# A 16-row bias product in the place of two zero products at the head of a two-layer trunk

## The chip, the cores and the metric

The kernel runs on one core of one Trainium2 chip, as one launch. The metric is the device time in microseconds (us); several executions of the same program are timed and the median stands for it. One more execution is recorded by the hardware profiler, and all rows of the trace come from that one. The core has a matrix engine (TensorE, PE in the rows; PEld is its weight load), VectorE (DVE), ScalarE (ACT), GpSimd (POOL) and SyncE (SP). Each has a queue of its own and waits on semaphores for the others. SyncE and ScalarE can both issue transfers from main memory.

## What is computed

256 tokens of width 1024 go through two layers in float32. Layer 0 has a stick-breaking attention and a SwiGLU. Layer 1 has an attention in three dilated groups over one shared set of keys and values, with a relative bias, and a SwiGLU. Cut to what the change touches:

```python
def shared_kv_from(x, g_kv, w_kv):
    kv = (rms_norm(x, g_kv) @ w_kv).reshape(b, s, N_GROUPS, 2, N_HEADS, HEAD_DIM)
...
def dilated_group_attention(qb, kk, vv, rel_bias, window, dilation):
    rel = Q_BLOCK + i - m
    bias = rel_bias[relative_bucket(rel * dilation)]
    bias = jnp.transpose(bias, (2, 0, 1))[:, None].astype(jnp.float32)
    s = jnp.einsum('brhnqd,brhnkd->brhnqk', qb.astype(jnp.float32), kk.astype(jnp.float32)) * scale + bias
    s = jnp.where(valid, s, NEG_INF)
    lse = jax.nn.logsumexp(s, axis=-1)
...
def reference(x, ...):
    for layer in range(DEPTH):
        h = rms_norm(x, g[0])
        h = mixer_a(...) if layer < N_A_LAYERS else mixer_b(...)
        x = x + rms_norm(h, g[1])
        h = swiglu(rms_norm(x, g[2]), w_gate_up[layer], w_down[layer])
        x = x + rms_norm(h, g[3])
```

`rel_bias` is a table of 32 buckets by 16 heads. The bias is needed in layer 1 only, whose attention begins near 310 us.

## The kernel before

**Staging.** Weights stream through three buffers (`raw`, "units" of up to 1 MB) that SyncE fills. ScalarE cuts each unit to its high part (`hi`, line 511, into `w_hi`), VectorE makes the rest (`lo`, line 800, into `w_lo`), and PE multiplies high by high, high by low and low by high, so that a float32 product becomes three fast ones. SyncE may load unit s only when unit s-3 is cut. The order on each engine is written out by hand; no scheduler changes it.

**The bias.** A one-hot matrix `select_in` (32 buckets by 512 distances) and the table `rel_in` (32 by 16) are loaded; one product on PE (line 1572, 16 by 512 in float32) picks the bias by head and distance, VectorE copies it to `bias_out` (line 1107), and GpSimd stores it to memory in two transfers (lines 482, 483), from where it is read back per head much later.

**The head of the program**, in the order of each engine:

- SyncE loads the identity `eye` (375), the two tiles of x (377), the first query and key weights (378 to 380), the first value unit (`half_values_a(0, 0)`), `ones` (382), the one-hot matrix (383) and the table (384), then two small matrices (385, 386) and further weights. The transfer of the second value unit waits for the first columns' products of the query, and the next query unit for those of the key.
- ScalarE loads the norm gains (705, 64 rows) and the gain of the shared norm (706, 8 rows), loads its function table (708), scales half of the turned x by the gains (713), rounds it (725) and then cuts units.
- PE multiplies zeros (`keep_busy(4)`, line 1551) from the moment that `rows` is cleared, turns tile 0 of x (1563), turns the gains (1560, after a wait for both gain transfers), turns tile 1, computes the first query and key columns straight from the float32 weights (`first_columns`, 1243), spreads the norm factors over rows (`spread_rows`, 1219), waits for the bias transfers, runs the bias product (1572), and goes on with the values (`values_a`, 1268 to 1271), the first scores (`scores_a`, 1252 and 1253), more values, the next query and key (`project_a`, 1197 to 1199) and the running sums of the attention (`sums_a`, 1285).
- VectorE squares x (1087), scales its half of the turned x (1080), makes the low part of x (1098), a diagonal (871), the first low weight part (800), the norm rows (876), query and key (921, 922), a second low part, and the bias copy (1107). An attention step has lines 900 to 905 there (its last, 905, is what `sums_a` waits for) and line 579 first on ScalarE, which waits for the scores.
- GpSimd computes the norm factors (422, 425) and then waits for `bias_out`.

The bias product writes to bank 3 of the PSUM memory, which the gains' transpose used before it and the scores use after it. Each bank holds 512 float32 columns, and the zero products write to bank 2, as the values do.

Of the kernel before, what the change touches and what calls it, by code (L numbers as in the profile page):

```python
# [32 lines left out]
NH = 16  # L33
# [9 lines left out]
BUCKETS = 32  # L43
# [58 lines left out]
def build(nc, x, norm_gains, w_qkv_a, w_o_a, g_kv, w_kv_b, w_q_b, w_o_b, rel_bias, w_gate_up, w_down,  # L102
# [16 lines left out]
    with ExitStack() as ctx:  # L119
# [3 lines left out]
        def sem(name):  # L123
            return ctx.enter_context(nc.semaphore(name))
# [28 lines left out]
        def carve(n, at=None):  # L153
            end[0] = (end[0] if at is None else at) + n
            assert end[0] <= WORK
            return work[:, end[0] - n:end[0]]
# [3 lines left out]
        select_in = carve(R * 2 * RUN)  # L160
        rel_in = carve(NH)
        mask_in = carve(WS)
        bias_out = carve(R * 2 * RUN)
# [48 lines left out]
        ps = ctx.enter_context(nc.psum_tensor("ps", [P, 8 * 512], F32))  # L212

        def bank(b, lo=0, n=512):
            return ps[:, 512 * b + lo:512 * b + lo + n]
# [5 lines left out]
        def banks(b, m, n):  # L221
# [10 lines left out]
        eye_in, ones_in, later_in, strict_in, gain_in_s, bias_in, mask_in_s = (sem(n) for n in (  # L232
            "eye_in", "ones_in", "later_in", "strict_in", "gain_in", "bias_in", "mask_in"))
# [3 lines left out]
        gain_done, gain_made, bias_done, bias_out_made, mask_made, expo_made = (sem(n) for n in (  # L237
            "gain_done", "gain_made", "bias_done", "bias_out_made", "mask_made", "expo_made"))
# [34 lines left out]
        def value_a(h):  # L273

            return A0 + (3 * h if h else 2)
# [45 lines left out]
        def _(sp):  # L321
# [58 lines left out]
            sp.dma_start(first_w[1], qkv_dram[:, 1, :, 0:P]).then_inc(first_in[2], 16)  # L380
            half_values_a(0, 0)
            sp.dma_start(ones[:, :], square[:, 3, :]).then_inc(ones_in, 16)
            sp.dma_start(select_in[0:BUCKETS, :], select).then_inc(bias_in, 16)
            sp.dma_start(rel_in[0:BUCKETS, :], rel_bias).then_inc(bias_in, 16)
            sp.dma_start(later, square[:, 1, :]).then_inc(later_in, 16)
            sp.dma_start(strict, square[:, 2, :]).then_inc(strict_in, 16)
            half_values_a(1, 0)
# [118 lines left out]
        def _(act):  # L506
# [176 lines left out]
            def swiglu_step(l, s0, i, j, units):  # L683

                s = s0 + 3 * i - 1
                for n, u in enumerate(units):
                    if n < NT and i == 1:
                        silu_of(l, s, i, j, n)
                    hi(u, j)
                    if n < NT and i > 1:  # L690
                        silu_of(l, s, i, j, n)

            def swiglu(l, s0, last_units):
# [8 lines left out]
                        swiglu_step(l, s0, i, j, range(s0 + 3 * i + 2, s0 + 3 * i + 5))  # L702
                swiglu_step(l, s0, STEPS - 1, 0, last_units)

            act.dma_start(gain_in[0:8 * KT, :], gain_rows).then_inc(gain_in_s, 16)
            act.dma_start(gain_in[8 * KT:9 * KT, :], g_kv.rearrange("(k p) -> k p", p=P)).then_inc(gain_in_s, 16)

# [88 lines left out]
        def _(dve):  # L796
            def lo(s, j=0):
                dve.wait_ge(hi_made, j * 6 + s + 1)
                n, c = size(s), s % CUT
                dve.tensor_tensor(w_lo[:, c, 0:n], raw[:, s % RAW, 0:n], w_hi[:, c, 0:n].bitcast(F32), ALU.subtract  # L800
                                  ).then_inc(lo_made, 1)
# [274 lines left out]
            def turned_x(b):  # L1076

                dve.wait_ge(xt_done, b + 1)
                for k in (2 * b, 2 * b + 1):
                    dve.tensor_scalar(xf[:, k, :], bank(4 + b, SEQ * (k % 2), SEQ), gains[:, k:k + 1], None, ALU.mult  # L1080
                                      ).then_inc(xf_dve, 1)
# [10 lines left out]
            dve.wait_ge(gain_made, 1)  # L1092
            turned_x(1)
            turned_x(3)
            for half in range(2):
                dve.wait_ge(xt_hi, 4 * NT * (half + 1))
                ks = slice(4 * half, 4 * half + 4)
                dve.tensor_tensor(xt[:, 1, ks, :], xf[:, ks, :], xt[:, 0, ks, :].bitcast(F32), ALU.subtract
                                  ).then_inc(xt_made, 4 * NT)
# [3 lines left out]
            take_rows(1)  # L1103
            take_qk_a(0, 0)
            lo(A0 + 3)
            dve.wait_ge(bias_done, 1)
            dve.tensor_copy(bias_out[0:NH, :], ps[0:NH, 3 * 512:4 * 512]).then_inc(bias_out_made, 1)
            lo(A0 + 4)
            lo(A0 + 5)
            dve.wait_ge(strict_in, 16)  # L1110
# [75 lines left out]
        def _(pe):  # L1186
            mm = nc.tensor.matmul
# [13 lines left out]
            def cut_unit(s, **dims):  # L1201
                n = size(s)
                spec = "p (k g n) -> p k g n" if "g" in dims else "p (k n) -> p k n"
                return [w[:, s % CUT, 0:n].rearrange(spec, **dims) for w in (w_hi, w_lo)]
# [11 lines left out]
            def spread_rows(use):  # L1216
                pe.wait_ge(diag_made, use)
                for t in range(NT):
                    inst = mm(bank(use, P * t, P), ones[:, :], ob[:, t, :], start=True, stop=True)
                inst.then_inc(rows_done, 1)  # L1220
# [25 lines left out]
            def scores_a(a, j):  # L1246
                pe.wait_ge(qka_made, j * 2 + a + 1)
                if a >= 1:
                    pe.wait_ge(arg_made, j * 2 + a)
                for hh in range(2):  # L1250
                    rows_ = slice(DH * hh, DH * hh + DH)
                    mm(bank(3 + hh, 0, SEQ), ka[rows_, 0:P], qa[rows_, :], start=True, stop=True)
                    inst = mm(bank(3 + hh, SEQ, P), ka[rows_, P:SEQ], qa[rows_, P:SEQ], start=True, stop=True)
                inst.then_inc(z_done, 1)

            def values_a(h, j, ks=range(4)):

                s, half = value_a(h), h % 2
                pe.wait_ge(lo_made, j * 6 + s + 1)
                if h == 0:  # L1260
                    pe.wait_ge(xt_made, KT * NT)
                elif not half:
                    pe.wait_ge(va_made, j + h // 2)
                w = cut_unit(s, k=4)
                for k in ks:
                    for t in range(NT):
                        out, xs = bank(2, 2 * P * t, 2 * P), [xt[:, n, 4 * half + k, P * t:P * t + P] for n in range(2)]
                        mm(out, xs[0], w[0][:, k, :], start=not half and k == 0 and t == 0, stop=False,  # L1268
                           skip_group_check=True)
                        mm(out, xs[0], w[1][:, k, :], start=False, stop=False, skip_group_check=True)  # L1270
                        inst = mm(out, xs[1], w[0][:, k, :], start=False, stop=half == 1 and k == 3, skip_group_check=True)  # L1271
                if k == 3:
                    inst.then_inc(w_used, 1)
# [275 lines left out]
            def keep_busy(n):  # L1549
                for _ in range(n):  # L1550
                    mm(bank(2, 0, SEQ), rows[:, 0:P], rows[:, :], start=True, stop=True)

            pe.wait_ge(zeros_made, 1)
            keep_busy(4)

            pe.wait_ge(eye_in, 16)
            for t in range(NT):
# [9 lines left out]
            first_columns(1)  # L1567
            pe.wait_ge(ones_in, 16)
            spread_rows(1)
            pe.wait_ge(bias_in, 32)  # L1570
            pe.wait_ge(gain_made, 1)
            mm(ps[0:NH, 3 * 512:4 * 512], rel_in[0:BUCKETS, :], select_in[0:BUCKETS, :],
               start=True, stop=True).then_inc(bias_done, 1)
            values_a(0, 0)
            pe.wait_ge(bias_out_made, 1)
            scores_a(0, 0)
            values_a(1, 0)
            pe.wait_ge(exact_made, 1)
# [89 lines left out]
```

## Time and profile before

| | us |
|---|---|
| median of 3 runs | 767.82 |
| lowest and highest of them | 766.83, 767.84 |
| profiled execution, its own time | 767.52 |
| span of the profiled execution, first to last instruction | 765.8 |
| PE busy in that span | 756.4 |
| DVE, ACT, POOL busy | 495.1, 418.2, 175.4 |

The profiled execution's own time is 1.7 us more than its span. A row of the order in time gives the start, the length (of one instruction, or of a run of equal ones up to the end of the last), the engine, the line of the kernel, the operation with its tiles and shape, how many, and in brackets how long the engine stood idle before it and what ended that. One float32 product on PE shows as two records.

### The profile page before, as it was taken

How to read it: one execution, taken by the hardware profiler on the slowest of the kernel's cores; microseconds unless marked ns; L12 is line 12 of the kernel's file. 1: busy time of each engine (PE TensorE's matmuls, PEld its weight loads, DVE VectorE, ACT ScalarE, POOL GpSimd, SP SyncE). 2: the span in 40 equal slices, each digit the busy share in tenths (PEclk: the TensorE clock that was granted, in tenths of full speed). 3: DMA queues.
4: the chain of work that ended last, by engine and by line, in shares of the span. 5: the costliest groups of instructions: out<-in, count | busy, mean ns of one | idle time of the engine just before them, and what ended most of it. 6: DMA issues, size and time to landing. Idle time of an engine off the chain costs nothing.

```text
span 765.8 us, 13552 instructions
## 1 busy us (share of the span) xinstructions
PE 756.4 (99%) x4731; PEld 650.9 (85%) x4731; DVE 495.1 (65%) x676; ACT 418.2 (55%) x633; POOL 175.4 (23%) x299
## 2 busy tenths in 40 slices
PE   9999999999999999999999999999999999999996
PEld 7999978888888888999899899898888888888884
DVE  5888987775455455777766667668647745544543
ACT  4766668443343443865866766767655444333421
POOL 2000001660000000236654765557002000000000
PEclk9999999999999999999999999999999999999999
DMA  8744674896655554659586795796634765566402
GB/s 251 207 123 145 220 224 161 250 255 209 209 183 164 181 189 123 166 157 243 153 205 171 177 230 151 177 240 161 210 138 151 262 196 187 176 213 208 170 1 55
DMA packets 160259, 139.62 MB, mean 182 GB/s; under 512 B 8152, under 2 KB 149056, under 8 KB 160224
## 3 DMA queue, kind: packets, MB, share of 16 engines
q1 hardware_dynamic: 153248, 131.45, 55.8%
q0 software_dynamic: 6784, 7.41, 5.5%
q8 instruction: 21, 0.34, 0.2%
q10 hardware_dynamic: 192, 0.30, 0.2%
q14 instruction: 14, 0.11, 0.0%
HBM read 138.02 MB, written 1.11 MB: 182 GB/s over the span
## 4 chain that ended last, share of the span: by engine, by line
PE 96%; DMA 2%; ACT 1%; DVE 1%; issue 0%; SPq 0%; POOLq 0%; POOL 0%; DVEq 0%
PE ps L1191 20%; PE ps L1193 20%; PE ps L1192 20%; PE ps L1441 10%; PE ps L1443 5%; PE ps L1197 3%; PE ps L1199 3%; PE ps L1198 3%; PE ps L1355 1%; DMA raw<-in_w_o_b 1%; PE ps L1268 1%; PE ps L1285 1%; PE ps L1270 1%; PE ps L1504 1%; PE ps L1271 1%; PE ps L1243 1%
## 5 line engine op out<-in xcount | busy, mean ns | idle before, releaser
L800 DVE TENSOR_TENSOR w_lo<-raw,w_hi 128x2048 fp32r<-128x2048 f32 (+2 forms) x144 | 280.6, 1964 | 41.8 <-ACT w_hi L511 39.3
L511 ACT ACTIVATE w_hi<-raw 128x2048 fp32r<-128x2048 f32 (+2 forms) x144 | 232.7, 1637 | 58.3 <-DMA raw<-in_w_kv_b 28.0
L1191 PE MATMUL ps<-w_hi,xt 128*128 128x512 f32 x352 | 139.6, 397 | 0.0
L1193 PE MATMUL ps<-w_hi,xt 128*128 128x512 f32 x352 | 137.3, 390 | 0.0
L1192 PE MATMUL ps<-w_lo,xt 128*128 128x512 f32 x352 | 137.0, 389 | 0.0
L680 ACT ACTIVATE work<-ps,stat 128x256 f32<-128x256 f32 x44 | 21.0, 477 | 199.5 <-PE ps L1193 199.5
L422 POOL TENSOR_SCALAR stat<-stat 128x1 f32<-128x1 f32 x16 | 9.9, 617 | 440.0 <-ACT work L527 416.0
L1191 PE MATMUL ps<-w_hi,ot 128*128 128x512 f32 x240 | 94.9, 395 | 0.4 <-ACT work L641 0.4
L1193 PE MATMUL ps<-w_hi,ot 128*128 128x512 f32 x240 | 93.5, 390 | 0.0
L1192 PE MATMUL ps<-w_lo,ot 128*128 128x512 f32 x240 | 93.5, 390 | 0.0
L1193 PEld LDWEIGHTS ps<-w_hi,xt 128*128 128x128 f32 x352 | 66.0, 188 | 14.1
L1191 PEld LDWEIGHTS ps<-w_hi,xt 128*128 128x128 f32 x352 | 66.1, 188 | 13.5 <-issue 0.6
L1192 PEld LDWEIGHTS ps<-w_lo,xt 128*128 128x128 f32 x352 | 66.2, 188 | 12.8
L452 POOL DMA_DIRECT2D work<-bias_rows x128 | 71.2, 557 | 13.8 <-POOL work L471 9.1
L1045 DVE CAST ot<-ps 128x512 fp32r<-128x512 f32 x22 | 15.2, 692 | 77.0 <-PE ps L1355 77.0
L1191 PEld LDWEIGHTS ps<-w_hi,ot 128*128 128x128 f32 x240 | 45.0, 188 | 10.6 <-ACT work L641 0.8
L1193 PEld LDWEIGHTS ps<-w_hi,ot 128*128 128x128 f32 x240 | 45.0, 188 | 9.6
L1192 PEld LDWEIGHTS ps<-w_lo,ot 128*128 128x128 f32 x240 | 45.1, 188 | 8.9
L641 ACT ACTIVATE work<-ps,stat 32x128 f32<-32x128 f32 x128 | 45.8, 358 | 1.5
L469 POOL TENSOR_TENSOR work<-mask_b,work 128x128 f32<-128x128 bf16 (+1 forms) x32 | 26.3, 822 | 84.4 <-DMA work<-bias_rows 72.4
L1038 DVE SCALAR_TENSOR_TENSOR work<-ps,stat,work 128x256 f32<-128x256 f32 x44 | 21.1, 479 | 35.6 <-ACT work L680 35.6
L964 DVE TENSOR_TENSOR work<-ps,ob 128x256 f32<-128x256 f32 x42 | 17.7, 421 | 39.9 <-ACT ob L623 39.7
(148 smaller groups left out, 1325.3 us busy)
## 6 DMA issues: line engine op xcount, KB each, us to landing
raw<-in_w_gate_up SPq DMA_DIRECT2D x88, 512.0 KB, 4.9
raw<-in_w_kv_b SPq DMA_DIRECT2D x96, 256.0 KB, 4.3
raw<-in_w_down SPq DMA_DIRECT2D x22, 1024.0 KB, 5.0
raw<-in_w_q_b SPq DMA_DIRECT2D x48, 256.0 KB, 4.0
raw<-in_w_qkv_a SPq DMA_DIRECT2D x23, 512.0 KB, 5.0
raw<-in_w_o_a SPq DMA_DIRECT2D x4, 1024.0 KB, 6.4
work<-bias_rows POOLq DMA_DIRECT2D x128, 32.0 KB, 3.8
raw<-in_w_o_b SPq DMA_DIRECT2D x4, 1024.0 KB, 6.0
```

What stands on the lines that cost most here:

```text
L452: pool.dma_start(band[at_, t].rearrange("p (c n) -> p c n", c=R), bands[r][ds(h, 1)][:, :, t].rearrange("h m c n -> (h m) c n")).then_inc( ...
L469: pool.tensor_tensor(to[0], blocked[0], distances[:, 0:t + 1], ALU.add)
L511: act.activation(w_hi[:, s % CUT, 0:size(s)], raw[:, s % RAW, 0:size(s)], ACT.Copy).then_inc(hi_made, 1)
L641: inst = act.activation(vown[p % 2][row:row + HR, r], src[tokens, g], ACT.Copy, scale=x_rs(2, t)[tokens])
L800: dve.tensor_tensor(w_lo[:, c, 0:n], raw[:, s % RAW, 0:n], w_hi[:, c, 0:n].bitcast(F32), ALU.subtract).then_inc(lo_made, 1)
L1191: mm(out, xs[0], ws[0], start=start, stop=False)
L1192: mm(out, xs[0], ws[1], start=False, stop=False)
L1193: return mm(out, xs[1], ws[0], start=False, stop=stop)
L1197: mm(out, ws[0], xs[0], start=start, stop=False)
L1198: mm(out, ws[0], xs[1], start=False, stop=False)
L1441: mm(both, w[k // 4][0][:, k % 4, g, :], x_[:, :, k, :], start=k == 0, stop=False, skip_group_check=True)
L1443: inst = mm(bank(b, 0, SEQ), w[k // 4][1][:, k % 4, g, :], x_[:, 0, k, :], start=False, stop=k == KT - 1, skip_group_check=True)
```

## The change

The two transfers of the one-hot matrix and the table leave SyncE's queue and come first on ScalarE's, ahead of the gains. On PE two of the four zero products go; the bias product stands behind the other two, ahead of the transposes of x, and now writes to bank 2. Its wait for the two transfers moves with it. VectorE's copy moves from behind the second low weight part up to before the low part of x. PE's wait for that copy now stands before the first values (which write bank 2 too); the wait for the gains stays ahead of the first scores.

```diff
@@ SyncE
             sp.dma_start(ones[:, :], square[:, 3, :]).then_inc(ones_in, 16)
-            sp.dma_start(select_in[0:BUCKETS, :], select).then_inc(bias_in, 16)
-            sp.dma_start(rel_in[0:BUCKETS, :], rel_bias).then_inc(bias_in, 16)
             sp.dma_start(later, square[:, 1, :]).then_inc(later_in, 16)
@@ ScalarE
+            act.dma_start(select_in[0:BUCKETS, :], select).then_inc(bias_in, 16)
+            act.dma_start(rel_in[0:BUCKETS, :], rel_bias).then_inc(bias_in, 16)
             act.dma_start(gain_in[0:8 * KT, :], gain_rows).then_inc(gain_in_s, 16)
@@ VectorE
             turned_x(3)
+            dve.wait_ge(bias_done, 1)
+            dve.tensor_copy(bias_out[0:NH, :], ps[0:NH, 2 * 512:3 * 512]).then_inc(bias_out_made, 1)
             for half in range(2):
...
             take_qk_a(0, 0)
             lo(A0 + 3)
-            dve.wait_ge(bias_done, 1)
-            dve.tensor_copy(bias_out[0:NH, :], ps[0:NH, 3 * 512:4 * 512]).then_inc(bias_out_made, 1)
             lo(A0 + 4)
@@ TensorE
             pe.wait_ge(zeros_made, 1)
-            keep_busy(4)
+            keep_busy(2)
+            pe.wait_ge(bias_in, 32)
+            mm(ps[0:NH, 2 * 512:3 * 512], rel_in[0:BUCKETS, :], select_in[0:BUCKETS, :],
+               start=True, stop=True).then_inc(bias_done, 1)
 
             pe.wait_ge(eye_in, 16)
...
             spread_rows(1)
-            pe.wait_ge(bias_in, 32)
+            pe.wait_ge(bias_out_made, 1)
+            values_a(0, 0)
             pe.wait_ge(gain_made, 1)
-            mm(ps[0:NH, 3 * 512:4 * 512], rel_in[0:BUCKETS, :], select_in[0:BUCKETS, :],
-               start=True, stop=True).then_inc(bias_done, 1)
-            values_a(0, 0)
-            pe.wait_ge(bias_out_made, 1)
             scores_a(0, 0)
```

How the instructions stand on TensorE at the start of the program (- before, + changed; `work` holds table, one-hot matrix and gains, and the zero products are line 1551):

```order
-L1551 MATMUL ps<-rows 128x256 x4
-L1563 MATMUL ps<-eye,xn 128x128 x8
-L1560 MATMUL ps<-eye,work 128x72
-L1563 MATMUL ps<-eye,xn 128x128 x8
+L1551 MATMUL ps<-rows 128x256 x2
+L1556 MATMUL ps<-work 16x512
+L1566 MATMUL ps<-eye,xn 128x128 x8
+L1563 MATMUL ps<-eye,work 128x72
+L1566 MATMUL ps<-eye,xn 128x128 x8
 L1243 MATMUL ps<-work,raw 128x256 x16
 L1219 MATMUL ps<-ob,ones 128x128 x2
-L1572 MATMUL ps<-work 16x512
```

The bias product went from behind `spread_rows` to behind two zero products, ahead of all transposes.

ScalarE's queue from its first instruction on:

```order
-L505 UNCONDITIONAL_BRANCH
+L503 UNCONDITIONAL_BRANCH
+L703 DMA work<-in_select 32x512
+L704 DMA work<-in_rel_bias 32x16
 L705 DMA work<-in_norm_gains 64x128
 L706 DMA work<-in_g_kv 8x128
```

The gains' transfers are now third and fourth on that queue.

VectorE between its part of the turned x (1080) and the first low weight part (800):

```order
 L1080 TENSOR_SCALAR work<-ps,gains 128x256 x4
-L1098 TENSOR_TENSOR xt<-work,xt 128x1024 x2
+L1096 COPY work<-ps 16x512
+L1100 TENSOR_TENSOR xt<-work,xt 128x1024 x2
 L871 TENSOR_SCALAR ob<-eye,stat 128x128 x2
 L800 TENSOR_TENSOR w_lo<-raw,w_hi 128x1024
```

The bias copy went ahead of the low part of x.

## Rows read from the trace of the kernel before

**Rows 1.** The page: busy time by engine, and the chain that ended last.
```profile
PE 756.4 (99%) x4731; PEld 650.9 (85%) x4731; DVE 495.1 (65%) x676; ACT 418.2 (55%) x633; POOL 175.4 (23%) x299
...
PE 96%; DMA 2%; ACT 1%; DVE 1%; issue 0%; SPq 0%; POOLq 0%; POOL 0%; DVEq 0%
```

**Rows 2.** Order in time on PE, 0 to 45 us.
```profile
1.32 3.64 PE L1551 MATMUL ps<-rows 128*128 128x256 f32 x8 [1.32 <-DVE rows L1075]
4.99 1.06 PE L1563 MATMUL ps<-eye,xn 128*128 128x128 f32 x8
5.89 0.23 PE L1560 MATMUL ps<-eye,work 72*128 72x72 f32 x1
6.25 1.09 PE L1563 MATMUL ps<-eye,xn 128*128 128x128 f32 x8
7.34 7.15 PE L1243 MATMUL ps<-work,raw 128*128 128x256 f32 x32
...
28.47 1.10 PE L1285 MATMUL ps<-xkv 128*128 128x512 f32 x6
```

**Rows 3.** Waits: engine, line, what it waited for, us, times, longest.
```profile
PEld ps L1563 <- DMA xn<-in_x: 0.3, 1, 0.3
```

**Rows 4.** One line's records (min/median/max ns); a stretch's busy times, last column GB/s.
```profile
L1551 PE MATMUL ps<-rows x8: 494/634/795, 1.3 to 4.5; 128*128 128x256 f32 x8
...
3.00:6.00 3.00, 2.97 (x14) 2.07 (x13) 1.12 (x1) 0.51 (x1) 0.00 (x0) 1.00 0.99 368
```

**Rows 5.** The chain that ended last, in order of time: start, length.
```profile
14.93 0.96 PE ps L1572 x2
```

**Rows 6.** Order in time on VectorE, 0 to 60 us.
```profile
7.41 1.66 DVE L1080 TENSOR_SCALAR work<-ps,gains 128x256 f32<-128x256 f32 x4
9.56 2.36 DVE L1098 TENSOR_TENSOR xt<-work,xt 128x1024 fp32r<-128x1024 f32 x2 [0.49 <-ACT xt L725]
...
12.70 1.23 DVE L800 TENSOR_TENSOR w_lo<-raw,w_hi 128x1024 fp32r<-128x1024 f32 x1 [0.38 <-ACT w_hi L511]
...
17.24 0.67 DVE L1107 COPY work<-ps 16x512 f32<-16x512 f32 x1
...
26.45 0.96 DVE L905 TENSOR_TENSOR xkv<-work,xkv 128x768 fp32r<-128x768 f32 x1
...
38.56 0.96 DVE L905 TENSOR_TENSOR xkv<-work,xkv 128x768 fp32r<-128x768 f32 x1
```

**Rows 7.** Order in time on ScalarE and its queue (ACTq), 0 to 60 us.
```profile
0.87 0.55 ACTq L705 DMA_DIRECT2D work<-in_norm_gains  x1
1.46 0.73 ACTq L706 DMA_DIRECT2D work<-in_g_kv  x1
...
20.24 1.06 ACT L511 ACTIVATE w_hi<-raw 128x1024 fp32r<-128x1024 f32 x1 [0.73 <-DMA raw<-in_w_qkv_a]
...
32.04 1.06 ACT L511 ACTIVATE w_hi<-raw 128x1024 fp32r<-128x1024 f32 x1 [0.47 <-DMA raw<-in_w_qkv_a]
33.35 0.81 ACT L579 ACTIVATE work<-ps 128x768 f32<-128x768 f32 x1 [0.26 <-PE ps L1253]
...
44.77 0.81 ACT L579 ACTIVATE work<-ps 128x768 f32<-128x768 f32 x1 [0.83 <-PE ps L1253]
```

**Rows 8.** Order in time on PE, 27 to 41 us: the next sums.
```profile
39.88 1.10 PE L1285 MATMUL ps<-xkv 128*128 128x512 f32 x6
```

**Rows 9.** Transfers: KB, us to landing; ScalarE's queue (q10), packets begun in 2.1:2.6 and 3.9:4.4.
```profile
xn<-in_x SPq DMA_DIRECT2D x1, 512.0 KB, 3.5
eye<-in_square SPq DMA_DIRECT2D x1, 64.0 KB, 1.8
...
work<-in_select SPq DMA_DIRECT2D x1, 64.0 KB, 4.7
...
q10 hardware_dynamic: 65, 0.03, 19.2%
...
q10 hardware_dynamic: 14, 0.00, 3.2%
```

## The prediction

> **What bounds the kernel now.** First the page: TensorE (PE) is busy for 756.4 of 765.8 us, and the chain that ended last runs through it for 96% [rows 1]. So a change counts only if it moves the time at which PE's work starts or ends. Next I read the head of the program on PE in order of time [rows 2], since every instruction that moves is issued before 18 us. PE multiplies zeros from 1.32 to 4.96, turns tile 0 of x (8 transposes from 4.99) and the gains (5.89), stands 0.3 us until tile 1 of x has landed, turns it (6.25 to 7.34), runs 32 records of the first query and key columns without a gap (7.34 to 14.49), spreads rows, runs the bias product (14.93 to 15.89), and then the values. From 7.34 on there is no gap.
>
> Two things set this head. One is the landing of x: PE goes straight from the zeros to tile 0, and its one named wait for a transfer is the 0.3 us for tile 1 [rows 3]. The other is TensorE's clock. Eight records of zeros take 3.64 us, 0.455 each; 32 records of the same shape at 7.34 take 7.15 us, 0.223 each [rows 2]. That is the half level (1.2 GHz) and the full one (2.4 GHz). A record's length tells the same: the median of the eight is 634 ns, the shortest 494 [rows 4]; the transposes that begin at 4.99 come 0.11 us apart for half the columns, at full pace. So the clock rose near 4.7, and PE had not stood still since 1.32. The removed zero products are what PE did while the clock rose.
>
> **The change, part by part.**
>
> *The bias product leaves the path behind the first columns.* In the chain it takes 0.96 us for its two records [rows 5]. Behind it the values need xt (VectorE L1098, over at 11.92) and the low part of their weights (12.70 + 1.23 = 13.93) [rows 6]; PE would be there at 14.93, a full us later. So 0.96 us goes from here.
>
> *How much of it arrives.* PE now comes 0.96 us earlier to waits on a chain that does not move: ScalarE's cut at 20.24 stood 0.73 us for a weight transfer, and the first attention step hangs behind that cut [rows 7]. At the sums (28.47) PE needs VectorE L905, over at 26.45 + 0.96 = 27.41: 1.06 to spare, by 0.1 us for weight load and semaphore some 0.9. At the next sums (39.88) it needs L905 of 38.56 + 0.96 = 39.52: 0.36 to spare, by the same 0.1 a good 0.2, and this chain can only come 0.26 us earlier, because ScalarE stood no longer than that for PE at 33.35, just after a cut that itself stood for a transfer at 32.04 [rows 6 to 8]. Together 0.45 us. In the steps after that ScalarE stands 0.83 us for PE at 44.77 [rows 7], so all follows PE and the 0.45 is kept. I take 0.45; the bounds are 0.4 and 0.96, the latter if the transfers also land earlier.
>
> *Two zero products go, the bias product comes.* By columns it is an exchange without a price: four records of 256 columns go, two of 512 come (32 rows to 16, which the trace shows to cost by columns: 0.96 us for two records at full clock, 0.48 each, about twice 0.223). At the half level I price it at 4 x 0.43 = 1.7 us. What is new is a wait. The two zero products left end near 3.1 (1.32 + 4 x 0.45); then PE stands until both the table and the one-hot matrix have landed.
>
> *When they land (L).* The trace shows no such transfer on ScalarE's queue. Nearest rows: the identity, 64 KB like the one-hot matrix and issued at 0.87 too, lands in 1.8 us; the first x tile, 512 KB and issued behind it, in 3.5; the one-hot matrix itself, on SyncE's queue amid other traffic at 7.1, in 4.7 [rows 9]. On ScalarE's queue now stand the gains (0.87) and g_kv (1.46); of its packets 65 start in 2.1 to 2.6 and the last 14 only in 3.9 to 4.4, when x fills the DMA engines [rows 7, 9]. The table is the second on that queue, as g_kv was. So L lies between 1.4 + 1.8 = 3.2 and 1.4 + 4.7 = 6.1, and I take 4.5, nearest to those last packets.
>
> With L = 4.5 and a clock that rises near 4.7 as before, the bias product is done by about 5.4 (0.2 us at the half level, the other 1.5 us of half-level work in 0.75), tile 0 and gains take 0.97 us to 6.4, and tile 1 can be turned from about 6.4.
>
> *The transfers ahead of x.* 66 KB now pass before x and not after it. At the 368 GB/s of 3 to 6 us [rows 4] that is 0.18 us later for tile 1 at most, nothing at least if they fit the gaps before 3 us. The Trainium skill, page DMA: Bandwidth & Descriptors, section Issuing engines are not separate DMA queues, says that transfers issued from different engines end on the same 16 DMA engines and that only issue time is saved. By that rule the 0.18 is due in full; if ScalarE's queue were a path of its own, it would be zero. The same page, section Anatomy of one DMA, gives about 2.0 us fixed plus size over 436 GB/s, for the software path; as an estimate by that page L would be 3.4, and the clock would hardly notice. The late packets in this trace speak against that.
>
> Head: tile 1 starts 0.18 us later, from either cause. I take +0.2.
>
> *The gains come later.* They are issued after the two new ones, about 1 us later (0.42 to 0.55 us each on the queue). PE needs them at 5.89 [rows 2], ahead of tile 1. Had g_kv needed as long as now (its last packets by 4.4), it would be there by about 5.4 to 5.9. Likely no cost, 0.9 us at worst.
>
> *VectorE and the rest.* The copy of the bias (16x512, 0.67 us at 17.24) moves between L1080, over at 9.07, and L1098, which stood 0.49 us for ScalarE until 9.56 [rows 6]. It is over at 9.7: 0.15 us late, taken up by the 0.38 us that VectorE stands before its cut at 12.70. The table load of ScalarE moves back by about 1 us with the two issues ahead of it, and nothing on ScalarE is due before the gains come out of PE at 5.89 + 0.23 [rows 2]. GpSimd's two stores of the bias follow the copy from about 18 to about 10, away from the transfer that the cut of 20.24 waits for. SyncE has two issues less. All at nothing; bounds -0.2 and +0.2.
>
> **Sum.** -0.45 + 0.2 = -0.25 us on the profiled execution's 767.52 (span 765.8 and 1.7 around it). The median of the runs shown is 767.82, 0.3 above it; from there I forecast 767.5.
>
> **Rivals.**
>
> *A, the forecast:* the clock rises about when it did. 767.2 to 767.8. For it: with L near 4.5 PE has worked from 1.32 to about 3.2 and works on from 4.5, so it is at work when the clock is due to rise. Against: in the trace it had no gap at all before the rise.
>
> *B, slower: the gap holds the clock down.* Place: PE between 3.1 and L. Price: the bias product ends at 4.5 + 1.7 = 6.2; tile 0 and the gains, 9 transposes at twice their 0.11 us, end at 8.1; if the clock is full from there, tile 1 ends at 9.0, where it was 7.2 before: +1.8 us, with -0.45 in all +1.4, 769.2. If it is half until 9.8, +2.6 less 0.45, 770.0. If the gap is short (L = 3.5) and the clock still late, about +1.2. It would decide from a gap of about 1 us on (L beyond 4), a point that I choose, as no row has one. For it: the packets of ScalarE's queue that only start at 3.9 to 4.4. Against: the execution shown has one instance of the rise only, and nothing says that so short a gap matters.
>
> *C: gains or bias are very late.* L = 5.5 with the clock full, or g_kv landed at 6.8: tile 1 waits 0.5 to 0.9 us, less 0.45: 767.8 to 768.3. It is the case that the trace bears out least.
>
> *D: all 0.96 us arrives,* because the transfer before the cut at 20.24 lands earlier without the stores beside it, and x is not delayed. Then 766.9. It would have to land half a us earlier, while ScalarE stood 0.73 us for it.
>
> **How the numbers follow.** About 0.2% (1.5 us) is what a measurement of this kernel can tell from no change. Chances: A 0.48, B 0.28, C 0.12, D 0.12. All of A and C is within 0.2%, as is D unless the runs lean that way. B lies on both sides of the bound: half of it over 1.5 us. That gives faster 0.05, same 0.79, slower 0.16. The range goes from 766.6 (D with the spread of the runs shown, 766.83 to 767.84) to 769.5, which takes in B up to its middle price and a little more.
>
> **What would show it.** After: two zero products, then a gap on PE that ends with a transfer as releaser, at L. Records of the bias product: near 0.9 us apart if half clock, 0.48 if full. Transposes of tile 0 at 0.11 us each: A; at 0.21: B. The start of the first columns, 7.34 before, should be 7.5 (A), 8.2 or later (B). The first columns to the first values should close up by 0.96 us. At 27.5 to 39.5 PE should show small waits for VectorE that the trace of before does not have; the start of the sums at 39.88 should move by 0.25 in A, by 0.75 in D. The prediction fails if the gap on PE is there and the clock has already risen in it, if tile 1 of x lands over 0.5 us later, or if the start at 39.88 moves by something other than the head's delay less 0.45.

## The result and the profile after

The changed kernel is slower: 769.24 us median (768.43 to 771.0, 14 executions) against 767.39 for the kernel before (766.78 to 769.39, 14 executions), a ratio of 1.0026 with a 95% interval from 1.0019 to 1.0033. The profiled execution has a span of 769.3 us; it is the slowest of the 14 (771.0), so its places are read here, and its size is not.

PE in order of time at the head (start, length, line, operation, count, idle before and what ended it), which answers to [rows 2]:

```profile
1.31 2.07 PE L1551 MATMUL ps<-rows 128*128 128x256 f32 x4 [1.31 <-DVE rows L1075]
4.67 1.88 PE L1556 MATMUL ps<-work 32*16 32x512 f32 x2 [1.28 <-DMA work<-in_rel_bias]
6.49 1.97 PE L1566 MATMUL ps<-eye,xn 128*128 128x128 f32 x8
8.24 0.33 PE L1563 MATMUL ps<-eye,work 72*128 72x72 f32 x1
8.37 1.80 PE L1566 MATMUL ps<-eye,xn 128*128 128x128 f32 x8
10.00 7.07 PE L1243 MATMUL ps<-work,raw 128*128 128x256 f32 x32
16.91 0.61 PE L1219 MATMUL ps<-ob,ones 128*128 128x128 f32 x4
17.27 0.36 PE L1268 MATMUL ps<-w_hi,xt 128*128 128x256 f32 x1
```

The gap is there, 1.28 us, and ends with the table at 4.67. Two records of the bias product take 1.88 us; in the same view they took 1.03 before (0.96 in the chain, [rows 5]). The first eight transposes take 1.97 where they took 1.06, and the first columns begin at 10.00, not 7.34: 2.66 us late. The length of single records (min/median/max, ns) shows when the clock rose:

```profile
L1556 PE MATMUL ps<-work x2: 1031/1044/1056, 4.7 to 5.5; 32*16 32x512 f32 x2
...
L1566 PE MATMUL ps<-eye,xn x16: 307/421/474, 6.5 to 9.9; 128*128 128x128 f32 x16
```

The median transpose takes 273 ns in the trace of before, at 2.4 GHz, and 421 here, at 1.2 GHz; only the last two, at 9.7 and 9.9, are shorter. The clock rose at about 9.9 instead of 4.7 [rows 4]. The profile's column of the granted clock says 1.00 in this stretch of both traces (3 to 5 us), so at the head of this program the level is told from the length of the records alone.

ScalarE's queue, which answers to [rows 7], and the transfers issued before 8 us with their time to landing [rows 9]:

```profile
0.87 0.42 ACTq L703 DMA_DIRECT2D work<-in_select  x1
1.33 0.44 ACTq L704 DMA_DIRECT2D work<-in_rel_bias  x1
1.81 0.53 ACTq L705 DMA_DIRECT2D work<-in_norm_gains  x1
2.37 0.72 ACTq L706 DMA_DIRECT2D work<-in_g_kv  x1
```
```profile
work<-in_select ACTq DMA_DIRECT2D x1, 64.0 KB, 2.2
...
work<-in_rel_bias ACTq DMA_DIRECT2D x1, 2.0 KB, 3.3
```

The one-hot matrix has landed at 3.1, the 2 KB of the table only at 1.33 + 3.3 = 4.6. In the changed kernel nothing is seen waiting for the gains, since PE comes to them only at 8.24: in this execution the slow clock hides them.

Further down, the attention sums of the second step, in order of time on PE, answer to [rows 8]:

```profile
41.71 1.19 PE L1285 MATMUL ps<-xkv 128*128 128x512 f32 x6
```

They began at 39.88 before, so of the 2.66 us at the first columns 1.83 are left: the shorter path gives back 0.83, or 0.75 if it is counted from the end of the first columns (17.07 for 14.49).

### The profile page after: what moved, and what is told of

Same layout as the page of the kernel before. It is cut to its first block, busy times and chain, and to the rows that moved or that the text cites. A ratio compares the mean times of both kernels' runs of the same rounds, so it can differ in the third digit from the quotient of the medians.

```text
span 769.3 us, 13543 instructions
## 1 busy us (share of the span) xinstructions
PE 757.7 (98%) x4727; PEld 651.5 (85%) x4727; DVE 494.2 (64%) x676; ACT 417.1 (54%) x633; POOL 172.5 (22%) x299
## 4 chain that ended last, share of the span: by engine, by line
PE 79%; ACT 5%; DMA 5%; issue 5%; DVE 4%; SPq 0%; ACTq 0%; POOLq 0%; POOL 0%; DVEq 0%
PE ps L1191 19%; PE ps L1193 19%; PE ps L1192 18%; DMA raw<-in_w_kv_b 3%; PE ps L1441 3%; ACT work L639 3%; PE ps L1197 3%; PE ps L1199 2%; PE ps L1198 2%; PE ps L1443 2%; DVE w_lo L800 2%; ACT w_hi L509 1%; PE ps L1355 1%; DVE work L964 1%; PE ps L1285 1%
## 5 line engine op out<-in xcount | busy, mean ns | idle before, releaser
L1441 PE MATMUL ps<-xt,w_hi 128*128 128x512 f32 x168 | 43.1, 398 | 0.5 <-ACT work L639 0.5
L1441 PE MATMUL ps<-xkv,w_hi 128*128 128x512 f32 x168 | 43.2, 399 | 0.0
```

The lines of the kernel that those rows point to most:

```text
L1441: mm(both, w[k // 4][0][:, k % 4, g, :], x_[:, :, k, :], start=k == 0, stop=False, skip_group_check=True)
```

## The experiments

All times are medians, of 5 to 14 executions for each kernel and of 14 to 33 for the kernel before beside it, on the same chip. The change of the median is in us. Most intervals reach 0.7 us to either side (0.0009 of 767), so two rows whose changes differ by less than about 1 us are not told apart by them alone.

| kernel | median | before | change | ratio, 95% interval |
|---|---|---|---|---|
| changed (result) | 769.24 | 767.39 | +1.85 | 1.0026, 1.0019 to 1.0033 |
| changed_again | 769.23 | 767.19 | +2.04 | 1.0024, 1.0015 to 1.0034 |
| four_zeros | 768.34 | 767.10 | +1.24 | 1.0016, 1.0007 to 1.0025 |
| before_two_zeros | 768.46 | 767.10 | +1.36 | 1.0017, 1.0008 to 1.0026 |
| before_transfers_first | 767.92 | 767.10 | +0.82 | 1.0011, 1.0002 to 1.0020 |
| before_no_bias_product | 766.85 | 767.10 | -0.25 | 0.9996, 0.9987 to 1.0005 |
| before_two_zeros_transfers_first | 769.39 | 767.31 | +2.08 | 1.0023, 1.0013 to 1.0032 |
| tables_cleared | 768.23 | 767.31 | +0.92 | 1.0009, 1.0001 to 1.0018 |
| cleared_128_columns | 768.36 | 767.19 | +1.17 | 1.0016, 1.0007 to 1.0025 |
| cleared_128_rows | 767.05 | 767.19 | -0.14 | 0.9997, 0.9988 to 1.0006 |
| changed_without_wait | 769.04 | 767.19 | +1.85 | 1.0021, 1.0012 to 1.0031 |
| transfers_on_gpsimd | 771.53 | 767.31 | +4.22 | 1.0052, 1.0039 to 1.0065 |
| transfers_on_gpsimd_four_zeros | 771.24 | 767.31 | +3.93 | 1.0042, 1.0028 to 1.0055 |
| full_rows | 768.54 | 767.39 | +1.15 | 1.0018, 1.0009 to 1.0027 |
| full_rows_four_zeros | 767.67 | 767.39 | +0.28 | 1.0006, 0.9997 to 1.0015 |

### One part of the change alone

**before_two_zeros**, the kernel before with fewer zeros:

```diff
-            keep_busy(4)
+            keep_busy(2)
```

> The kernel before with two zero products instead of four and nothing else. PE then stands from about 3.2 until tile 0 of x at 4.9. Theory (gap): the clock rises late, transposes 0.21 us apart, first columns begin at 8.5 to 9.5 instead of 7.34, and 768.6 to 769.9 in all, since nothing is given back behind. Rival 1 (transfers) and rival 2 (kind of product): no change, 767.2 to 767.6, clock up by 5.

PE in order of time:

```profile
4.78 1.94 PE L1563 MATMUL ps<-eye,xn 128*128 128x128 f32 x8 [1.39 <-DMA xn<-in_x]
...
8.34 7.35 PE L1243 MATMUL ps<-work,raw 128*128 128x256 f32 x32
```

The eight transposes take 1.94 us, at the half level; the first columns begin 1.0 us late and end 1.2 us late. +1.36 us: the two zero products had a use, and theory gap holds for this kernel, though the median lies just below the range that it gave.

**before_transfers_first**, the kernel before with the two bias transfers first on ScalarE's queue:

> The kernel before with the two bias transfers first on ScalarE's queue, and nothing else. Theory (gap): the clock is as before; tile 1 of x lands at 6.7 as in the changed kernel and not 6.2, the gains at 6.9 to 7.2, so PE starts tile 1 at 6.9 to 7.2 and 767.9 to 768.4 comes out, a third of the loss. Rival 1 (transfers): all of the loss, 769.2. Third case, transfers do not matter: 767.4.

```profile
5.06 1.06 PE L1563 MATMUL ps<-eye,xn 128*128 128x128 f32 x8 [0.17 <-DMA xn<-in_x]
7.39 0.28 PE L1560 MATMUL ps<-eye,work 72*128 72x72 f32 x1 [1.26 <-DMA work<-in_g_kv]
...
8.52 7.17 PE L1243 MATMUL ps<-work,raw 128*128 128x256 f32 x32
```

The clock is up as before (1.06 for eight transposes). PE stands 1.26 us for `in_g_kv`, the fourth transfer of the queue, a wait that the kernel before does not have. +0.82 us, as expected. No delay of x is shown: tile 0 is turned at 5.06 for 4.99, but traces without these transfers ahead of x have it at 4.78 (before_two_zeros), 5.13 (before_no_bias_product) and 5.79 (tables_cleared). Of the 1.2 us at the first columns 0.5 is left in the span (766.3 for 765.8). The rest goes in layer 1, where the kernel before has PE stand for ScalarE, in the waits of PE's weight load (us in total, times, longest):

```profile
PEld ps L1191 <- ACT work L641: 0.8, 1, 0.8
```

This row is missing in the same waits of before_transfers_first and before_two_zeros. It is there in those of before_no_bias_product (0.7), changed (1.4) and changed_again (1.1), so being early or late at the head does not settle it, and its cause is open. Nor do the medians show that a loss at the head shrinks towards the end: in before_two_zeros 1.2 us at the first columns stand beside +1.36. The spans of single traces are therefore not used as sizes here.

**before_no_bias_product**, the kernel before without the late product (the bias is cleared instead):

```diff
-            mm(ps[0:NH, 3 * 512:4 * 512], rel_in[0:BUCKETS, :], select_in[0:BUCKETS, :],
-               start=True, stop=True).then_inc(bias_done, 1)
...
-            dve.wait_ge(bias_done, 1)
-            dve.tensor_copy(bias_out[0:NH, :], ps[0:NH, 3 * 512:4 * 512]).then_inc(bias_out_made, 1)
+            dve.memset(bias_out[0:NH, :], 0.0).then_inc(bias_out_made, 1)
```

> The kernel before without the bias product: VectorE clears the bias instead of copying it, so that layer 1 runs without a relative bias. It shows what the shorter path behind the first columns is worth with the head left alone. All theories: 0.4 to 0.96 us faster, most likely 0.7 as read from the changed kernel's trace (2.6 us later at the first columns' end, 1.9 at the third attention step); 766.7.

-0.25 us, within the interval no change, and less than the 0.4 to 0.96 that was expected. In its trace x landed a little later, and the first columns and the second sums stand at

```profile
7.56 7.17 PE L1242 MATMUL ps<-work,raw 128*128 128x256 f32 x32
...
39.39 1.22 PE L1284 MATMUL ps<-xkv 128*128 128x512 f32 x6
```

+0.22 and -0.49 against [rows 2, 8]: of the 0.96 us 0.71 arrives there. By the medians 0.25 us is what taking the product off this path wins in all, and that is not clear of zero.

**before_two_zeros_transfers_first**, both edits in the kernel before:

> The kernel before with both: two zero products, and the bias transfers first on ScalarE's queue; the bias product stays late. Theory G (both causes, but they lie over one another, since slow transposes and the wait for the gains fill the same time before tile 1): first columns begin at 8.5 to 9.5, and 768.2 to 769.2, less than the sum of the single losses of 0.8 and 1.4 us (769.3). Theory S (they add up): 769.3 or more. As the bias product stays late, it should lie 0.3 us or so over the changed kernel's path gain and without its slow product: if the early product at half clock is what makes the changed kernel the slowest, this one stays under 769.

+2.08, about the sum of the two (2.18). The median is 0.1 us above the 769.3 from which theory S begins and 0.2 above the range of theory G: it speaks for S, but within the noise. In its trace PE comes to the gains only at 7.01 and stands 0.1 us before them, and what is lost is in the clock: the first columns begin at 8.89 and take 8.27 us, against 7.35 in before_two_zeros. Why the clock rises later there is open. With the product in its late place this kernel loses as much as the changed one (+1.85, +2.04): an early product of 32 rows is worth no more there than standing still.

### One part of the change undone

**four_zeros**, the changed kernel with `keep_busy(4)`:

> The changed kernel with four zero products again instead of two; the bias product still stands behind them, and the transfers are still on ScalarE's queue. Theory (the gap that PE has while it waits for the table holds the clock down): zeros run to about 5.0, the table has landed at 4.6 by the trace of the changed kernel, so there is no gap, the clock rises near 5 as in the kernel before, the bias product takes 0.9 to 1.2 us, tile 1 of x is turned from about 6.9 (6.25 before, 8.37 changed), and of the 0.7 us that the shorter path behind gives back all but nothing is left: 767.0 to 767.8 against 767.4 for the kernel before. Rival 1 (the transfers ahead of x are to blame): tile 1 is late as now, 768.5 or more. Rival 2 (a product of 32 rows to 16 does not hold or raise the clock as the zeros do): the transposes are 0.21 us apart again, 769 or more.

```profile
4.82 1.03 PE L1556 MATMUL ps<-work 32*16 32x512 f32 x2
5.78 1.09 PE L1566 MATMUL ps<-eye,xn 128*128 128x128 f32 x8
7.37 0.28 PE L1563 MATMUL ps<-eye,work 72*128 72x72 f32 x1 [0.50 <-DMA work<-in_g_kv]
```

In this execution (767.44) all was as the theory had it: no gap, full clock, and only the gains late. But the median is 768.34, between the theory (767.8 at most) and its rivals (768.5 or more), and the 11 executions spread over 2.4 us: five from 767.25 to 767.82, six from 768.34 to 769.67. No trace shows one of the slow six. The gap was not all, so two more causes were tested.

**transfers_on_gpsimd** and **transfers_on_gpsimd_four_zeros**, where GpSimd issues the two transfers:

```diff
-            act.dma_start(select_in[0:BUCKETS, :], select).then_inc(bias_in, 16)
-            act.dma_start(rel_in[0:BUCKETS, :], rel_bias).then_inc(bias_in, 16)
+            pool.dma_start(select_in[0:BUCKETS, :], select).then_inc(bias_in, 16)
+            pool.dma_start(rel_in[0:BUCKETS, :], rel_bias).then_inc(bias_in, 16)
```

> The changed kernel with its two bias transfers on GpSimd's queue, so that the gains are the first on ScalarE's again and land by 4.9; two zero products. The gap is the only cause left. They should land between 3.5 and 5. If the gap matters: clock up at 6 to 9, slow product, tile 1 at 7.2 to 8.4, 767.8 to 768.8. If the late gains were the whole loss of the changed kernel: 766.4 to 767.0.

> The same with four zero products: neither a gap nor late gains, only the product between zeros and tile 0. The zeros end at 5.0, the product takes 0.9 to 1.0 us at full clock, tile 1 begins at 6.9 instead of 6.25, and 0.6 us comes back behind: 766.9 to 767.4, no change against the kernel before. If it stays at 768 or more, something that neither cause names is at work.

```profile
7.34 1.88 PE L1556 MATMUL ps<-work 32*16 32x512 f32 x2 [3.95 <-DMA work<-in_rel_bias]
```

They missed their aim, and their expectations by 3 to 4 us: the table, issued at 2.11, took 5.2 us to land, so the gap became 3.95 us (1.81 with four zeros) and the loss 4 us. They say nothing of the gains. In the trace of the kernel with four zeros their use is lost over the wait behind them:

```profile
6.91 1.88 PE L1556 MATMUL ps<-work 32*16 32x512 f32 x2 [1.81 <-DMA work<-in_rel_bias]
8.72 1.97 PE L1566 MATMUL ps<-eye,xn 128*128 128x128 f32 x8
```

The zeros end at 5.10 with their last record still at the half level (634 ns), and the product and the transposes behind the gap are at the half level too. That is one execution (772.05); the eight lie between 768.76 and 772.62.

The Trainium skill, page DMA: Bandwidth & Descriptors, section SWDGE vs HWDGE vs iDMA, calls the path of SyncE and ScalarE faster in its setup than GpSimd's; by that rule, the trace agrees in the direction: 3.3 us for the table from ScalarE, 5.2 from GpSimd. How much of that is the setup it does not show, since GpSimd also issued 0.8 us later, beside other traffic.

**tables_cleared**, the changed kernel without its transfers; VectorE clears both tiles, and PE's wait asks for that (1 instead of 32):

```diff
-            act.dma_start(select_in[0:BUCKETS, :], select).then_inc(bias_in, 16)
-            act.dma_start(rel_in[0:BUCKETS, :], rel_bias).then_inc(bias_in, 16)
...
+            dve.memset(select_in[0:BUCKETS, :], 0.0)
+            dve.memset(rel_in[0:BUCKETS, :], 0.0).then_inc(bias_in, 1)
```

> The changed kernel without its two bias transfers: VectorE clears table and one-hot matrix behind the zeros, so the early bias product multiplies zeros and layer 1 runs without a relative bias. No gap on PE and nothing ahead of the gains. If the gap and the late gains are the whole loss, what is left is the shorter path: tile 1 at about 6.3, 766.4 to 766.9 against 767.1 for the kernel before. If the early product itself does harm (its shape, or the clock under it), transposes at 0.21 us and 768 or more.

```profile
1.32 2.08 PE L1551 MATMUL ps<-rows 128*128 128x256 f32 x4 [1.32 <-DVE rows L1073]
3.32 1.88 PE L1556 MATMUL ps<-work 32*16 32x512 f32 x2
5.79 1.94 PE L1566 MATMUL ps<-eye,xn 128*128 128x128 f32 x8 [0.59 <-DMA xn<-in_x]
```

No gap until 5.2, then 0.59 us for x, no late gains, and yet the transposes are at the half level and it is +0.92 us. The early product does not do for the clock what the removed zeros did. That it does harm is not shown: before_two_zeros, which stands still in its place, is at +1.36.

**cleared_128_columns** and **cleared_128_rows** are tables_cleared with one size of that product changed each; the number of moving columns stays (the second diff takes out the same two lines):

```diff
-            mm(ps[0:NH, 2 * 512:3 * 512], rel_in[0:BUCKETS, :], select_in[0:BUCKETS, :],
-               start=True, stop=True).then_inc(bias_done, 1)
+            mm(ps[:, 2 * 512:3 * 512], rows[0:BUCKETS, 0:P], select_in[0:BUCKETS, :],
+               start=True, stop=True).then_inc(bias_done, 1)
```
```diff
+            mm(bank(2, 0, SEQ)[0:NH, :], rows[:, 0:NH], rows[:, :], start=True, stop=True)
+            mm(bank(2, SEQ, SEQ)[0:NH, :], rows[:, 0:NH], rows[:, :], start=True, stop=True).then_inc(bias_done, 1)
```

> As tables_cleared (768.2, clock up at 10.8 in its trace although PE had no gap before 5.2; no bias transfers, layer 1 without a bias), but the early product has 128 stationary columns instead of 16, on the same 32 rows and with the same 512 moving columns. Theory P (a product that uses little of the array does not raise the clock as the zeros do, and it is the columns): clock up by 5.5 in most executions, transposes 0.11 us apart, 766.7 to 767.2 against 767.2 for the kernel before. If it is the rows, or the place or the wait and not the shape: 768.0 or more, as tables_cleared.

> As tables_cleared, but the early product uses 128 rows and 16 stationary columns, in two products of 256 moving columns, whose halves fill the bank; all zeros. If it is the rows: 766.7 to 767.2. If it is the columns: 768.0 or more. If both count, between, about 767.6.

cleared_128_columns, then cleared_128_rows:

```profile
5.32 1.97 PE L1566 MATMUL ps<-eye,xn 128*128 128x128 f32 x8
7.08 0.33 PE L1563 MATMUL ps<-eye,work 72*128 72x72 f32 x1
7.20 1.52 PE L1566 MATMUL ps<-eye,xn 128*128 128x128 f32 x8
```
```profile
5.38 1.93 PE L1566 MATMUL ps<-eye,xn 128*128 128x128 f32 x8 [0.17 <-DMA xn<-in_x]
7.12 0.26 PE L1563 MATMUL ps<-eye,work 72*128 72x72 f32 x1
7.22 1.04 PE L1566 MATMUL ps<-eye,xn 128*128 128x128 f32 x8
```

It is the rows. With 32 rows to 128 columns: +1.17 us. With 128 rows to 16 columns: -0.14, and 11 executions within 766.48 to 767.40, as close together as those of the kernel before. All 22 executions of the two cleared kernels with 32 rows lie above them (767.42 to 769.33, and 767.51 to 769.16 in tables_cleared). In the traces the clock is up near 7.0 with 128 rows, near 8.1 with 128 columns (its fastest execution) and near 10.7 in tables_cleared. The theory had the columns; that was wrong. The product of 128 rows is also cut into two of 256 columns, where the others have one of 512; the next kernel has that cut with 32 rows and is slow, so the cut is not what helps.

**changed_without_wait**, the changed kernel whose early product reads zeros and does not wait; 32 rows, transfers in place:

> The changed kernel with its two transfers where they are, first on ScalarE's queue, but an early product that does not wait for them: it multiplies zeros (32 rows to 16, two of 256 columns), and layer 1 runs without a relative bias. It takes the gap on PE away from the changed kernel and keeps the narrow product and the late gains. If the gap is the larger part of the loss: 767.9 or less (late gains alone cost 0.8, the path gives 0.3 to 0.6 back). If the narrow product keeps the clock down anyway: 768.3 to 768.9, 0.4 to 0.9 less than the changed kernel.

+1.85, only 0.2 less than changed_again beside it, a little over the upper case. Filling the gap with a narrow product wins nothing that can be measured, which fits tables_cleared: 32 rows do for the clock about as little as standing still. In this trace PE stands 0.82 us for `in_g_kv` as well, and the first columns begin at 9.87 and take 8.59 us, so the clock is up only near 12.9.

**changed_again**:

> The changed kernel as it is, on the same chip as the three beside it, as their measure: 769.0 to 769.5. Its trace gives a second instance of the rise of the clock: late again (8 or later) by all theories.

All 16 transposes are at the half level here:

```profile
L1566 PE MATMUL ps<-eye,xn x16: 421/421/474, 6.5 to 9.9; 128*128 128x128 f32 x16
```

### The changed kernel with a product over all rows

**full_rows** computes the bias as the changed kernel does. Rows 32 to 127 of both tiles are cleared and multiplied too:

```diff
             dve.memset(rows[:, :], 0.0).then_inc(zeros_made, 1)
+            for lo_, hi_ in ((32, 64), (64, 128)):
+                dve.memset(select_in[lo_:hi_, :], 0.0)
+                inst = dve.memset(rel_in[lo_:hi_, :], 0.0)
+            inst.then_inc(zeros_made, 1)
...
-            mm(ps[0:NH, 2 * 512:3 * 512], rel_in[0:BUCKETS, :], select_in[0:BUCKETS, :],
+            pe.wait_ge(zeros_made, 2)
+            mm(ps[0:NH, 2 * 512:3 * 512], rel_in, select_in,
```

**full_rows_four_zeros** has `keep_busy(4)` besides.

> The changed kernel, complete, whose bias product uses all 128 rows: VectorE clears rows 32 to 127 of table and one-hot matrix beside the zero products, and the product has the same result over 128 rows instead of 32. Gap (until 4.6) and late gains (7.3) stay. If the narrow product is the larger part of the loss and the gap a small one: 767.9 to 768.4, 0.9 to 1.3 below the changed kernel (769.2). If a gap of 1.3 us keeps the clock down just as well: 768.8 to 769.3, no gain, as the kernel before with two zero products and the transfers first (769.4 against 767.3).

> The same with four zero products: no gap, a product over all rows, only the late gains left. They alone cost 0.8 us in the kernel before, the shorter path gives 0.3 to 0.6 back: 767.3 to 767.8, against 768.3 (767.3 to 769.7, widely spread) for the changed kernel with four zero products and the narrow product. The spread should close up to that of the kernel before. If it stays at 768.3 with its wide spread, the rows are not the cause here.

```profile
5.16 1.89 PE L1561 MATMUL ps<-work 128*16 128x512 f32 x2 [1.78 <-DMA work<-in_rel_bias]
6.98 1.97 PE L1571 MATMUL ps<-eye,xn 128*128 128x128 f32 x8
```

That is full_rows. Its median is 0.14 us above the range for a narrow product as the larger part, and below the other case; full_rows_four_zeros is in its range, and spreads over 1.6 us where four_zeros spreads over 2.4. The product costs the same over 128 rows as over 32 at the same level (1.89 and 1.88 us), so rows are free in time. Together with the two kernels of 32 rows this is a square, in us against the kernel before:

| | two zeros | four zeros |
|---|---|---|
| product over 32 rows | +1.85, +2.04 | +1.24 |
| product over 128 rows | +1.15 | +0.28 |

By the medians rows are worth 0.7 to 1.0 us in either column, the two zero products 0.6 to 0.9 in either row. Each of these differences is within the noise of its two rows, and they come from several chips; that rows count rests on the cleared kernels, and the square points the same way. The trace of full_rows alone would not show it: its clock is up near 9.6, in the changed kernel's traces near 9.9 and 10.8. Nor is the +0.28 read from a trace: in that of full_rows_four_zeros PE does not stand for the gains, but the bias product is still at the half level (1.84 us), the transposes behind it at the full one.

## Why the prediction was wrong

The forecast was 767.5, 0.25 us won, which is no change that can be measured; 1.85 us were lost, clear of the noise. That 769.24 is inside the range (766.6 to 769.5) is owed to rival B, for which the range was stretched, not to the forecast's mechanism. By its own steps:

- **The view of the head was right.** The landing of x and the clock set it, and the removed zeros were what PE did while the clock rose: before_two_zeros, +1.36 us.
- **When the table lands:** forecast 4.5, 4.6 in the trace. Right as a number; the reason given, second on the queue while x fills the engines, fits but was not tested. In full_rows the same transfer took 3.8 us, to 5.1.
- **How much of the 0.96 us arrives:** forecast 0.45; 0.71 at the second sums without the product and 0.83 in the changed kernel. Less than 0.96 arrives, as said, and within the bounds given (0.4 to 0.96), but 0.45 was too low; which of the waits in that sum was overrated was not tested. At the end the product's absence is worth 0.25 us by the medians.
- **"By columns it is an exchange without a price" is the step that failed, and with it "a clock that rises near 4.7 as before".** In time it is an exchange: 1.88 us at the half level, near what was priced (1.7). For the clock it is not. It rose at about 9.9 and 10.8 in the two traces of the changed kernel. Without the two zero products alone the loss is 1.36 us, and a product over 32 of 128 rows in their place does not give it back (+0.92, where 128 rows give -0.14; 0.7 to 1.0 us in the full kernels). No rival had the rows. Rival B named the gap as what holds the clock down. That is part of it, as before_two_zeros and the kernels with the transfers on GpSimd show, but closing the gap with a narrow product is worth 0.2 us. The +0.2 taken for the head was 2.66 in the profiled execution.
- **"The gains come later ... likely no cost" failed too.** They were to be there by 5.4 to 5.9. In before_transfers_first PE waits for them until 7.39, 1.26 us, and 0.82 us come out at the end. Rival C had a price near this one (0.5 to 0.9 us) and took it as what the trace bears out least. In the changed kernel's own traces no wait for the gains is seen, because PE is late by then for the other cause.
- **x behind the bias transfers:** forecast +0.2, neither borne out nor refuted. VectorE's first square, which waits for tile 0, starts at 4.90 to 5.17 in the eight traces with these transfers first on ScalarE's queue, and at 4.67 to 5.68 in the six with none ahead of x. A shift of 0.2 us is lost in that.
- **Rival B as a number** was right, in part by luck: 769.2 forecast, 769.24 measured. It counted +1.4 from 767.82, where +1.85 from 767.39 was measured, and it had neither the rows nor the late gains in it. Its chance of 0.28 was too low, as the trace had only ever shown the rise after uninterrupted zeros, and the forecast took an interrupted and narrower stretch as good enough.
- Left open: in the profiled execution of the changed kernel the span is 3.5 us longer, though only 1.8 of it is there at 42 us. The rest arises in layer 1, where ScalarE stands longer for weight transfers (6.7 us for 5.1 between 420 and 435) and PE's weight load longer for ScalarE (1.4 for 0.8); that one causes the other is not shown. It is the slowest of 14 executions, and no experiment was made on it.

## What to carry to other kernels

By this one kernel, work that fills PE while its clock is low must also be work that lets the clock rise: if real work takes the place of filler, give it all 128 rows (zero rows cost no time) and let no wait stand in front of it. What goes first on a transfer queue at the start can push the last of that queue back: here two transfers put first made PE wait 1.26 us for the fourth. So look for who waits for the last one. A gain of less than a microsecond behind the head is not worth the risk to the head: the most to win here was 0.25 us, and no version of the early product came out ahead of the kernel before by more than its interval.

## What the runs showed of the hardware

- TensorE's clock rises later after a product over 32 rows than after one over 128, with equal moving columns and equal time: 768.23 and 768.36 us (32 rows, 16 and 128 stationary columns) against 767.05 (128 rows, 16 columns); in their traces it is up near 10.7, 8.1 and 7.0. The number of stationary columns made no difference that can be told from these runs.
- At the half level the time of a product does not depend on the rows: 1.88 us for 32 and 1.89 for 128 (two records, 512 columns, 1.2 GHz). The Trainium skill, page TensorE: Matmul & The Clock Gate, section Why this matters for your kernels, says the same of a product over 32 rows; the trace agrees.
- The instant of the rise differs between executions of one kernel (the transposes of the changed kernel were full at the very end in one execution and at no time in another), and so do the times: 768.15 to 770.60 in changed_again, 766.76 to 767.82 for the kernel before beside it. Medians of ten executions were needed to see effects of 1 us.
- Four zero products and then 1.81 us of standing: the product and the transposes that follow are at the half level (one trace, transfers_on_gpsimd_four_zeros). Without the standing the transposes are at the full one (before, four_zeros, full_rows_four_zeros).
- 2 KB issued at 1.33 us on ScalarE's queue took 3.3 us to land, while 64 KB issued before it took 2.2.
